# A two-layer decoder trunk: the middle folds of the down projection take both activation parts in one matmul, squares are summed by transfers, and VectorE makes the first weight sum

## What is computed

```
def rmsnorm(x, g):
    xf = x.astype(jnp.float32)
    y = xf * lax.rsqrt(jnp.mean(xf * xf, axis=-1, keepdims=True) + EPS)
    return (y * g.astype(jnp.float32)).astype(x.dtype)

def swiglu(h, w_gate_up, w_down):
    gu = h @ w_gate_up
    g, u = gu[..., :D_FF], gu[..., D_FF:]          # D_FF = 2816
    return (jax.nn.silu(g) * u) @ w_down
...
    for layer in range(DEPTH):                     # DEPTH = 2
        h = h + mixer(rmsnorm(h, ...))
        h = h + memory_cross_attention(rmsnorm(h, ...), rmsnorm(mem, ...), ...)
        h = h + swiglu(rmsnorm(h, ffn_norm[layer]), ffn_w_gate_up[layer], ffn_w_down[layer])
    return rmsnorm(h, final_norm)
```

## Time and profile before

| | us |
|---|---|
| median of three runs | 1381.32 (1381.27 to 1384.84) |
| the profiled execution | 1377.28 |
| its span | 1375.6 |
| TensorE busy in the span | 1364.1 |
| VectorE busy | 1021.5 |
| ScalarE busy | 700.9 |
| GpSimd busy | 203.7 |

### The profile page before, as it was taken

How to read it: one execution, slowest core, us unless ns; L and a number is a source line. 1 busy time by engine, 2 the same in 40 slices (tenths; PEclk the granted TensorE clock), 3 DMA queues, 4 the chain that set the end, 5 groups by cost and what they waited for, 6 DMA issues and landing times.

```text
span 1375.6 us, 21278 instructions
## 1 busy us (share of the span) xinstructions
PE 1364.1 (99%) x8048; PEld 1200.9 (87%) x8048; DVE 1021.5 (74%) x1447; ACT 700.9 (51%) x1056; POOL 203.7 (15%) x191
## 2 busy tenths in 40 slices
PE   9999999999999999999999999999999999999997
PEld 8988888889999988998887888988888999998997
DVE  6656556469789899985668855755558978899985
ACT  6633534355455556443756635534445455557342
POOL 0012200110122200231111211100020122210031
PEclk9999999999999999999999999999999999999998
DMA  9721320223667755354221212542032477764342
GB/s 343 272 91 63 107 91 33 92 78 107 176 178 181 194 146 139 112 164 169 92 92 47 77 47 77 178 159 77 31 100 68 146 182 185 187 177 143 106 150 77
DMA packets 54461, 176.56 MB, mean 128 GB/s; under 512 B 6624, under 2 KB 7136, under 8 KB 54240
## 3 DMA queue, kind: packets, MB, share of 16 engines
q1 hardware_dynamic: 38592, 136.79, 29.4%
q0 software_dynamic: 12032, 28.32, 10.4%
q10 hardware_dynamic: 3744, 10.17, 2.1%
HBM read 173.16 MB, written 2.10 MB: 127 GB/s over the span
## 4 chain that ended last, share of the span: by engine, by line
PE 92%; DVE 3%; issue 2%; DMA 1%; ACT 1%; POOL 0%; POOLq 0%; DVEq 0%; ACTq 0%; SPq 0%
PE acc L2437 15%; PE acc L2439 15%; PE acc L2438 15%; PE acc L2762 8%; PE acc L2767 7%; PE acc L2765 3%; PE acc L2766 3%; PE acc L2485 3%; PE acc L2486 3%; PE acc L2487 3%; PE aux L2762 2%; DMA raw<-in_weights 1%; PE aux L2816 1%; PE aux L2818 1%; PE aux L2819 1%
## 5 line engine op out<-in xcount | busy, mean ns | idle before, releaser
L1477 DVE TENSOR_TENSOR w_lo<-raw,w_hi 128x1024 fp32r<-128x1024 f32 (+1 forms) x149 | 181.3, 1218 | 97.1 <-ACT w_hi L743 96.8
L743 ACT ACTIVATE w_hi<-raw 128x1024 fp32r<-128x1024 f32 (+1 forms) x149 | 153.0, 1029 | 81.8 <-PE acc L2439 40.7
L2437 PE MATMUL acc<-u_hi,w_hi 128*128 128x512 f32 x352 | 138.9, 395 | 0.0
L2439 PE MATMUL acc<-u_hi,w_lo 128*128 128x512 f32 x352 | 137.4, 390 | 0.0
L2438 PE MATMUL acc<-u_lo,w_hi 128*128 128x512 f32 x352 | 137.2, 390 | 0.0
L2767 PE MATMUL acc<-b_both,w_lo 128*128 128x256 f32 x432 | 122.2, 283 | 0.0
L2767 PE MATMUL acc<-b_both,s_lo 128*128 128x256 f32 x432 | 121.8, 282 | 0.0
L2762 PE MATMUL acc<-b_both,s_hi 128*128 128x512 f32 x336 | 121.3, 399 | 0.0
L1341 POOL TENSOR_TENSOR sqsum<-sqsum,tmp 128x512 f32<-128x512 f32 x40 | 58.0, 1450 | 344.2 <-ACT tmp L752 322.8
L2437 PE MATMUL acc<-y_hi,w_hi 128*128 128x512 f32 x256 | 100.2, 391 | 0.0
L2439 PE MATMUL acc<-y_hi,w_lo 128*128 128x512 f32 x256 | 99.8, 390 | 0.0
(11 more groups left out here) (358 smaller groups left out, 3911.7 us busy)
## 6 DMA issues: line engine op xcount, KB each, us to landing
raw<-in_weights SPq DMA_DIRECT2D x253, 512.0 KB, 3.3
memT<-in_weights POOLq DMA_DIRECT2D x56, 256.0 KB, 4.9
raw<-in_weights POOLq DMA_DIRECT2D x28, 256.0 KB, 3.8
raw<-in_weights POOLq DMA_DIRECT2D x8, 512.0 KB, 5.4
hT<-in_x_t ACTq DMA_DIRECT2D x4, 512.0 KB, 7.0
x_tok<-in_x ACTq DMA_DIRECT2D x4, 512.0 KB, 4.9
memT<-in_weights POOLq DMA_DIRECT2D x4, 512.0 KB, 5.6
raw<-in_weights SPq DMA_DIRECT2D x5, 256.0 KB, 5.7
```

The source lines that it names most:

```text
L743: act.activation(w_hi[:, s, c], raw[:, s, c], ACT.Copy).then_inc(hi_ready, 1)
L1477: dve.tensor_tensor(w_lo[:, s, c], raw[:, s, c], w_hi[:, s, c].bitcast(F32), ALU.subtract)\
L2437: pe.matmul(out, w_h, x_h, start=first, stop=False)
L2439: return pe.matmul(out, w_l, x_h, start=False, stop=last)
```

## The change

In five of the eight folds (`fold_wide`: folds 1, 2 and 3 of layer 0, folds 1 and 2 of layer 1) a product takes the high and the low activation part in one matmul of 512 columns, as the pair steps do. It writes a whole PSUM bank: high x high into the first half, high x low into the second, and the third matmul, low x high, adds to the second half. The two halves of a bank are added behind it: copies and quarter sums are 512 wide, and each residual add is done in two instructions (`fold_add_wide`). `fold_both` and `fb_both` name the same memory as the four tensors that they replace. `fold_copy` waits for quarter 21 of the fold before in every case, and copies of wide folds go to `tmp[:, 2]`, `tmp[:, 3]` and `rstd_row`.

The first weight sum `t_pre` is made by VectorE behind `fold_mid` (`fold_pre`), and GpSimd's `pre_sum` is gone. `fold_lo_part(i + 1, 7)` goes from ahead of quarter 11 to behind quarter 22. The squares of tiles 1 to 5 are added to `sqsum` by accumulating transfers that GpSimd issues one after the other (`square_sums`); only tiles 6 and 7 of layer 0 are still added by its own instructions. GpSimd's queue becomes `third_sum(0)`, `(1)`, `(2)`, square 1, `third_sum(3)`, squares 2 to 5.

```
+        def fold_wide(layer, i):
+            return 0 < i < FOLDS - layer
+        def fold_moving(m, k):
+            if m in (7, 5, 6):
+                return fb_both[:, :, (7, 5, 6).index(m), k, :]
+            return fold_both[:, :, k + (0 if m in (1, 4) else KT), half(1 if m in (3, 4) else 0)]
...
-                        pe.matmul(out, hi[:, w], x_h, start=(k == 0 and (m in (1, 2, 7) or m == 3 and alone)), stop=False,
-                                  skip_group_check=True)
-                        pe.matmul(out, hi[:, w], x_l, start=False, stop=False, skip_group_check=True)
+                        first = k == 0 and (m in (1, 2, 7) or m == 3 and alone)
+                        if fold_wide(layer, i):
+                            pe.matmul(fold_bank(layer, i, m)[:, :], hi[:, w], fold_moving(m, k), start=first, stop=False,
+                                      skip_group_check=True)
+                            out = fold_part(layer, i, m, 1)
+                        else:
+                            pe.matmul(out, hi[:, w], x_h, start=first, stop=False, skip_group_check=True)
+                            pe.matmul(out, hi[:, w], x_l, start=False, stop=False, skip_group_check=True)
                         ins = pe.matmul(out, lo[:, w], x_h, start=False, stop=(k == KT - 1), skip_group_check=True)
...
-                        act.wait_ge(fquarter_ready, fold_quarter_at(layer, i - 1, {1: 11, 6: 21, 7: 22}[m]))
+                        act.wait_ge(fquarter_ready, fold_quarter_at(layer, i - 1, 21))
...
                     if j >= 3:
-                        act.wait_ge(sq_added, (KT - 1) * (norm - 1) + j - 2)
+                        act.wait_ge(square_in, squares_in(layer, j - 2))
...
-                for i in range(1, FOLDS):
-                    pre_sum(layer, i)
-                    if i + 1 < FOLDS:
-                        third_sum(layer, i + 1)
-                    if i < FOLDS - 1:
-                        add_squares(norm, 2 * i, max(1, 2 * i - 2))
-                add_squares(norm, KT if layer == 0 else KT - 2, KT - 4)
+                third_sum(layer, 2)
+                square_sums(layer, 1, 2)
+                third_sum(layer, 3)
+                square_sums(layer, 2, 6)
...
+            def square_sums(layer, j0, j1):
+                for j in range(j0, j1):
+                    if j > 1:
+                        pool.wait_ge(square_in, squares_in(layer, j - 1))
+                    pool.wait_ge(sq_ready, 8 * (3 * layer + 2) + j + 1)
+                    pool.dma_start(sqsum[:, :], tmp[:, j % 2, :], accum_op=ALU.add).then_inc(square_in, 16)
...
+                def fold_pre(i):
+                    dve.wait_ge(mid_ready, mid_at(layer, i))
+                    dve.wait_ge(fshi_ready, fold_sums_at(layer, i - 1, 5))
+                    x = fold_unit(layer, i, 1)
+                    dve.tensor_tensor(t_pre, t_mid, raw[:, x % RING, :], ALU.subtract).then_inc(lo_ready, 2)
...
-                            dve.wait_ge(sq_added, (KT - 1) * (norm - 1) + 2 * i - 1)
+                            dve.wait_ge(square_in, squares_in(layer, 2 * i - 1))
...
+                def fold_add_wide(i, c):
+                    j = 2 * i + (c == 20)
+                    e = {11: half(0), 20: slice(0, S), 12: half(1)}[c]
+                    out, op = hT[:, j, e], ALU.subtract if c == 20 else ALU.add
...
+                    k = step(dve.tensor_tensor(out, out, parts[0], op))
+                    dve.wait_ge(dve_step, k)
+                    dve.tensor_tensor(out, out, parts[1], op).then_inc(fold_added, 1)
...
                 fold_mid(1)
+                fold_pre(1)
                 fold_quarter(0, 21)
...
                         fold_lo_part(i + 1, 1)
                         fold_sum_lo(i, 3)
-                        fold_lo_part(i + 1, 7)
...
                     fold_quarter(i, 22)
                     if not last:
+                        fold_lo_part(i + 1, 7)
                         fold_mid(i + 1)
+                        fold_pre(i + 1)
                         fold_lo_part(i + 1, 2)
```

More of the change, by code:

```diff
@@ L609, in fold_bank, with fold_part, fold_sum_copy, squares_in @@
             return auxs[e] if (i + layer) % 2 else accs[(F_ACC[layer] + A_DN + e) % 4]
-        def fold_part(layer, i, m):
-            return fold_bank(layer, i, m)[:, 0:S // 2]
+        def fold_part(layer, i, m, e=0):
+            return fold_bank(layer, i, m)[:, half(e)]
+        def fold_wide(layer, i):
+            return 0 < i < FOLDS - layer
+        def fold_sum_copy(layer, i, m):
+            if fold_wide(layer, i):
+                return {1: tmp[:, 2, :], 6: tmp[:, 3, :], 7: rstd_row[:, :]}[m]
+            return {1: copy_1, 6: copy_u, 7: copy_7}[m]
+        def fold_moving(m, k):
+            if m in (7, 5, 6):
+                return fb_both[:, :, (7, 5, 6).index(m), k, :]
+            return fold_both[:, :, k + (0 if m in (1, 4) else KT), half(1 if m in (3, 4) else 0)]
+        def squares_in(layer, j):
+            return 16 * (5 * layer + j)
         def fold_half(m):
@@ L1038, in fold_copy @@
                     if i:
[L1039 removed]
+                        act.wait_ge(fquarter_ready, fold_quarter_at(layer, i - 1, 21))
                     else:
                         act.wait_ge(quarter_ready, quarters_at(layer, PAIRS - 1))
[L1042 to L1043 removed]
+                    src = fold_bank(layer, i, m)[:, :] if fold_wide(layer, i) else fold_part(layer, i, m)
+                    act.activation(fold_sum_copy(layer, i, m), src, ACT.Copy).then_inc(fcopied, 1)
                 def down_square(j):
@@ L2009, in fold_quarter @@
                     dve.wait_ge(fcopied, fold_copy_at(layer, i, of))
-                    copy = {11: copy_1, 21: copy_u, 22: copy_7}[c]
-                    dve.tensor_tensor(tmp[:, c // 20, half(1 if c == 22 else 0)], fold_part(layer, i, m), copy, ALU.add)\
-                        .then_inc(fquarter_ready, 1)
+                    wide = fold_wide(layer, i)
+                    if wide and c == 21:
+                        dve.wait_ge(fold_added, folded(layer, i - 1) + 1)
+                    dst = tmp[:, 1 if c == 22 else 0, :] if wide else tmp[:, c // 20, half(1 if c == 22 else 0)]
+                    src = fold_bank(layer, i, m)[:, :] if wide else fold_part(layer, i, m)
+                    dve.tensor_tensor(dst, src, fold_sum_copy(layer, i, of), ALU.add)\
+                        .then_inc(fquarter_ready, 1)
+                def fold_add_wide(i, c):
+                    j = 2 * i + (c == 20)
+                    e = {11: half(0), 20: slice(0, S), 12: half(1)}[c]
+                    out, op = hT[:, j, e], ALU.subtract if c == 20 else ALU.add
+                    if c == 11:
+                        dve.wait_ge(fquarter_ready, fold_quarter_at(layer, i, 11))
+                        parts = [tmp[:, 0, half(h)] for h in range(2)]
+                    elif c == 20:
+                        dve.wait_ge(fquarter_ready, fold_quarter_at(layer, i, 21))
+                        out = out.rearrange("p (a t) -> p a t", a=2)
+                        parts = [tmp[:, 0:2, half(h)] for h in range(2)]
+                    else:
+                        dve.wait_ge(fold_done, fold_at(layer, i, 3))
+                        parts = [fold_part(layer, i, 3, h) for h in range(2)]
+                    k = step(dve.tensor_tensor(out, out, parts[0], op))
+                    dve.wait_ge(dve_step, k)
+                    dve.tensor_tensor(out, out, parts[1], op).then_inc(fold_added, 1)
                 def fold_add(i, c):
+                    if fold_wide(layer, i):
+                        return fold_add_wide(i, c)
                     j = 2 * i + c // 20
```

35 lines of the change are left out of this document (19 added, 16 removed).

## The result

The changed kernel takes 1399.24 us in the median of 6 runs (1397.64 to 1401.95), the kernel before 1381.3 beside it (1377.27 to 1384.84, 6 runs). The ratio is 1.0141, with a 95% interval of 1.0121 to 1.0162; the two medians alone give 1.0130. So it is slower by 1.3 to 1.4%. I had forecast 1382.9 us, with a range up to 1389.5. The profiled execution took 1397.69 us with a span of 1396.0, against 1377.28 and 1375.6 before: 20.4 us more. (One thing in the description of the change is the other way round in the code: the low activation part stands first in `fold_both` and `fb_both`, so high x low goes into the first half of the bank and high x high into the second. For the time it makes no difference.)

What follows compares the result with a forecast made beforehand. TensorE, busy 99% of the span, was taken as the bound. Gains of 4.10 us against losses of 5.7 gave net +1.6 on 1381.32, so 1382.9 us, range 1376.5 to 1389.5.

Steps and rivals of the forecast that it cites:

- merged products: Five wide folds, 280 places: one 512-column matmul replaces two, 0.3533 us a group against 0.360, saving 1.74 us in all.
- small and large holes of before: TensorE's holes at product 6 of folds 1 (0.40, 0.39 us) and product 3 of fold 2, layer 0 (1.57) close.
- fold 2, layer 0: Product 3 waits for quarter 22, behind two square transfers landing after 5.6 and 4.8 us: hole of 1.7 us (0 to 3).
- fold 3, layer 0: Squares 4 and 5 start 7.4 us in, landing after 3.8 + 4.8 us; quarter 22 1.1 us late (0 to 4.2).
- fold 2, layer 1: Same order as fold 2 of layer 0: a new hole of 1.7 us (0 to 3).
- fold 3, layer 1: Turns wait for fold 2's adds, 1.0 us; later quarter 11 delays the sum inside product 5, 0.2 us (0 to 3.8).
- The holes at product 6: In folds 1 of both layers, VectorE's first sum ends the slowing beside GpSimd, so holes of 0.40 and 0.39 us close.
- The place of the risk: Square transfers, awaited by quarter 11 ahead of quarter 22 and product 3, could take back all the gain.
- The rival on the slower side, both transfers slow: Both square transfers of a fold take 5.8 us each; folds 2, fold 3 and tail wait: +10.5, 1391.8 us; chance 0.19.
- Folds 1 wait for a single transfer: In folds 1 one square transfer, issued 7.8 us in, lands by 13.6, before the 14.9 needed: no loss.
- The 1.57 us at product 3 of fold 2: Layer 0: moving the split behind quarter 22 stops a late accumulating transfer holding quarters 11 and 22, gaining 1.57 us.
- VectorE's additions, costed at nothing: Wide folds: wider quarter sums, doubled residual adds and first sum add 3.5 us a fold, hidden in VectorE's waiting time.

## Why the prediction was wrong

| term | as predicted | as measured in the two profiles |
|---|---|---|
| merged products | -1.74 | -1.74, and -0.7 more |
| small and large holes of before | -2.36 | -2.36 |
| fold 1, layer 0 | 0 | +2.78 |
| fold 2, layer 0 | +1.7 | +3.30, clock +1.51 |
| fold 3, layer 0 | +1.1 | +3.88, clock +2.33 |
| fold 0, layer 1 | 0 | +1.18 |
| fold 1, layer 1 | 0 | +2.33, clock +1.59 |
| fold 2, layer 1 | +1.7 | +3.52, clock +1.59 |
| fold 3, layer 1 | +1.2 | +0.79 |
| sum | +1.6 | +20.0 of 20.4 |

*Right.* No stage outside the down projections moved by more than 0.3 us. The merged groups start 0.353 to 0.354 us apart in three of the five folds and 0.347 in the two that follow a product at the lower clock. The holes at product 6 are gone, and `t_lo` takes 1.22 us. The place of the risk was right too: the transfers decide, at product 3, through quarter 11. The rival on the slower side, both transfers slow, named that mechanism; at +10.5 us it was still half of what came.

*The step that failed first* is "Folds 1 wait for a single transfer, issued 7.8 us in and landed by 13.6, early enough (14.9)". Its data were ready 7.96 us into the fold (568.85). But `third_sum(2)` had left 0.6 us before; square 1 was issued 13.0 us in and found landed 17.4 us in. I had put the transfer behind third_sum into the sum of folds 2 and left it out of folds 1. The run with more memory for descriptors shows that the transfer ahead, and not the square's own time of issue, sets the 10 us. Counted from the issue of the weight transfer ahead, I had 6.8 us in folds 2 (592.1 less 585.3) and no term in folds 1; measured are 10.06 us in fold 1 (578.28 less 568.22) and 8.41 in fold 2 (598.13 less 589.72).

*The second* is that I costed each fold as though the others ran on time. From quarter 11 to the last residual addition it is 12.0 us (578.28 to 590.32, predicted 11.6), and the squares wait for that addition. A late quarter 11 holds TensorE at product 3, and the next fold begins as soon as that product is done, and its squares come late. Weight transfer and square 2 of fold 2 were issued 6.2 and 8.1 us into it, where I had 4.8 and 6.0. So a hole hands itself on. The landings of fold 2 themselves cost no more than I had put: 6.1 and 3.3 us from issue, 9.4 together, in layer 0, and 7.6 and 3.2, 10.8 together, in layer 1, against 5.6 and 4.8, 10.4 together. The kernel without the merger shows the loop from the other side: it has less between quarter 11 and the squares and lies 11 us below the changed one, 7 more than the 4.0 that the merger costs without transfers.

*The third* is the clock. A hole was costed at its own length. Four of the five were followed by a product at the lower level of the clock, 7.0 us together, a term the prediction did not have.

*Fold 3* was nearly right in the time of its squares (4 and 5 issued 6.7 and 10.6 us into the fold), but the second took about 6.4 us, 618.76 to 625.17, where I had 4.8. A step was missing as well: in this fold VectorE makes a split for the mixer between quarters 11 and 22, in the kernel before as after, which puts quarter 22 1.1 us further back. Its timeline:

```profile
625.17 0.69 DVE L2047 TENSOR_TENSOR tmp<-aux,tmp 128x512 f32<-128x512 f32 x1 [5.57 <-DMA sqsum<-tmp]
...
626.70 1.22 DVE L1502 TENSOR_TENSOR w_lo<-raw,w_hi 128x1024 fp32r<-128x1024 f32 x1
627.83 0.68 DVE L2047 TENSOR_TENSOR tmp<-aux,rstd_row 128x512 f32<-128x512 f32 x1
```

*Credit for the wrong edit.* The 1.57 us at product 3 of fold 2 was put down to the moved split; it belongs to VectorE's sum. And VectorE's additions, costed at nothing because they are hidden, are hidden only in folds that do not end a layer.

Two sizes stay open: the late weights in fold 0 of layer 1 (1.18 us here; ScalarE waited 4.33 us for a unit ahead of the fold, 3.1 in the kernel before), seen only in kernels with merged matmuls in five folds and not in every layer of those, and 0.4 us of the sum.

## What to carry to other kernels

Before an engine's own 1.5 us addition is handed to a transfer, ask who waits for the landing and what is ahead in the same queue: here the landing came 8 to 11 us after the issue of the transfer ahead, even where it was issued 4.3 us sooner, and with two matmuls everywhere, giving the squares buffers of their own, so that quarter 11 need not wait, took the whole cost away. Cost a stall on TensorE above its length, since the clock can fall behind it, and follow it once around the loop, since a late step makes the next fold's step late. When several edits are bundled, time each alone: here one was worth 0.3%, one paid only in three places of five, one did nothing, and one cost more than all of them gave.

## What the runs showed of the hardware

- In the six kernels whose quarter 11 waits for square transfers, 25 holes at product 3 were of 1.95 us or more (up to 7.03, with 512 bytes), in a stream at 2.4 GHz. Behind 22 of them the product ran mostly at 1.2 GHz and took 4.2 to 5.3 us. The length alone does not decide it: behind one of 1.95 us (square transfers alone) the product took 4.45 us, behind 2.78 (the changed kernel), 2.72 (1536 bytes) and 2.39 us (512 bytes) the clock stayed at 1.00. It also stayed there behind 2.09 and 2.26 us at turned tiles (squares by additions, merged matmuls alone). Behind holes up to 1.74 us in the down projections and just after them it never fell.
- After such a product the merged groups of the next fold started 0.347 us apart (2.77 us a product) in six of nine cases, where 0.354 is usual. The kernel with merged matmuls alone has 0.347 in much of its layer 0 as well, with no product at the lower clock ahead. No run tells why.
- With 1024 bytes a partition for descriptors GpSimd held one square transfer of a layer for 4.6 to 7.9 us; with 512 bytes both that follow a weight transfer and 26 transfers of the pair steps, 3.3 to 5.1 us each, and the kernel took 46 us more than with 1024 (1444.79 against 1399.24); with 1536 none was held. A held square left 0.2 to 0.4 us after the weight transfer ahead of it had landed, also where that took 8.5 us instead of 5.1 to 5.6.
